# A mixture-of-experts step in split fp32: gate and up units of all four experts ahead of the down units, hidden rows turned two experts at a time

## The reference, cut to what matters

```python
gsel = jnp.argmax(glog, axis=-1)                    # one group of 4 experts for a token
gate = jnp.sum(one_hot(eidx, N_EXPERTS) * (gw * top_p)[..., None], axis=1)
hid = silu(einsum('nd,edf->nef', x, w_g)) * einsum('nd,edf->nef', x, w_u)     # d = 1024, f = 256
y = einsum('nef,efd->nd', hid * gate[..., None], w_d)
```

## Time and profile before

| what | value |
|---|---|
| median of 3 runs | 1677.16 us (1676.7 to 1677.43) |
| profiled execution, its own time | 1681.39 us |
| its span in the trace | 1679.8 us |
| TensorE busy | 98% of the span |
| VectorE, ScalarE busy | 59%, 51% of the span |

### The profile page before, as it was taken

How to read it: one execution, slowest core, us unless ns; L and a number is a source line. 1 busy time by engine, 2 the same in 40 slices (tenths; PEclk the granted TensorE clock), 3 DMA queues, 4 the chain that set the end, 5 groups by cost and what they waited for, 6 DMA issues and landing times.

```text
span 1679.8 us, 26741 instructions
## 1 busy us (share of the span) xinstructions
PE 1651.4 (98%) x9997; PEld 1337.1 (80%) x9997; DVE 996.9 (59%) x1662; ACT 862.5 (51%) x1455; POOL 642.7 (38%) x408
## 2 busy tenths in 40 slices
PE   8999999999999999999999999999999999999998
PEld 7788887777888887777778888777778888877776
DVE  3137567564451179999860384765634503999997
ACT  2443344544443347888644343554445333588884
POOL 0644454335467711000125455543345766100002
PEclk9999999999999999999999999999999999999999
DMA  9723343353556569999865233333354564799994
GB/s 353 268 89 110 107 151 128 105 181 140 191 206 244 210 217 398 391 375 379 309 228 188 101 117 121 130 120 144 138 182 162 199 242 160 267 407 376 383 368 161
DMA packets 128112, 367.23 MB, mean 219 GB/s; under 512 B 12028, under 2 KB 42364, under 8 KB 128000
## 3 DMA queue, kind: packets, MB, share of 16 engines
q1 hardware_dynamic: 93872, 319.80, 51.7%
q10 hardware_dynamic: 27504, 21.74, 4.1%
q0 software_dynamic: 6624, 24.18, 3.8%
HBM read 341.71 MB, written 23.97 MB: 218 GB/s over the span
## 4 chain that ended last, share of the span: by engine, by line
PE 84%; DVE 8%; ACT 2%; issue 2%; DMA 2%; POOL 1%; SPq 1%; POOLq 0%; DVEq 0%; ACTq 0%
PE G L1391 20%; PE G L1393 19%; PE G L1392 19%; PE S L1391 3%; PE S L1393 3%; PE S L1392 3%; DVE wlo L1930 2%; DVE pA L1930 2%; PE T L1717 2%; PE O L1467 2%; PE O L1748 2%; PE S L1703 2%; DMA x_scratch<-pA 2%; DVE prob L1930 1%; PE T L1621 1%
## 5 line engine op out<-in xcount | busy, mean ns | idle before, releaser
L856 POOL TENSOR_TENSOR wlo<-raw,whi 128x1024 fp32r<-128x1024 f32 x198 | 489.0, 2475 | 558.1 <-ACT whi L1005 557.9
L1391 PE MATMUL G<-whi,hhi 128*128 128x512 f32 (+1 forms) x1440 | 578.4, 402 | 10.3 <-DVE wlo L1930 5.5
L1393 PE MATMUL G<-whi,hlo 128*128 128x512 f32 (+1 forms) x1440 | 558.3, 388 | 0.0
L1392 PE MATMUL G<-wlo,hhi 128*128 128x512 f32 (+1 forms) x1440 | 557.8, 387 | 0.0
L1391 PEld LDWEIGHTS G<-whi,hhi 128*128 128x128 f32 x1440 | 271.0, 188 | 85.6 <-issue 16.4
L1393 PEld LDWEIGHTS G<-whi,hlo 128*128 128x128 f32 x1440 | 270.8, 188 | 57.5
L1392 PEld LDWEIGHTS G<-wlo,hhi 128*128 128x128 f32 x1440 | 271.6, 189 | 46.8
L1005 ACT ACTIVATE whi<-raw 128x1024 fp32r<-128x1024 f32 x204 | 214.8, 1055 | 98.6 <-PE G L1393 66.5
L1930 DVE TENSOR_TENSOR wlo<-raw,whi 128x1024 fp32r<-128x1024 f32 x150 | 181.7, 1225 | 13.3 <-ACT whi L1013 9.2
L1013 ACT ACTIVATE whi<-raw 128x1024 fp32r<-128x1024 f32 x144 | 152.5, 1060 | 28.6 <-PE G L1393 16.5
L1930 DVE TENSOR_TENSOR wlo<-pA,whi 128x1024 fp32r<-128x1024 f32 x72 | 88.0, 1225 | 29.3 <-ACT whi L1013 24.5
(11 more groups left out here) (405 smaller groups left out, 2292.1 us busy)
## 6 DMA issues: line engine op xcount, KB each, us to landing
raw<-in_units SPq DMA_DIRECT2D x423, 512.0 KB, 5.1
pA<-in_units SPq DMA_DIRECT2D x78, 512.0 KB, 5.9
pB<-in_units SPq DMA_DIRECT2D x72, 512.0 KB, 6.1
h_sorted<-sig POOLq DMA_DIRECT2D x12, 514.0 KB, 6.4
hs<-h_sorted POOLq DMA_DIRECT2D x10, 514.0 KB, 7.3
y_sorted<-yo POOLq DMA_DIRECT2D x10, 512.0 KB, 6.9
bias<-in_nat_bias ACTq DMA_DIRECT2D x16, 256.0 KB, 3.4
pB<-rows_scratch ACTq DMA_DIRECT2D x8, 512.0 KB, 9.1
```

Source lines behind the costliest of these rows:

```text
L856: lo_done.of(nc.gpsimd.tensor_tensor(wlo[:, k, :], raw[:, POS_OF[g] % RAW, :], whi[:, k, :].bitcast(F32), ALU.subtract))
L1391: nc.tensor.matmul(dst, st_hi, mv_hi, start=start, stop=False)
L1392: nc.tensor.matmul(dst, st_hi, mv_lo, start=False, stop=False)
L1393: return nc.tensor.matmul(dst, st_lo, mv_hi, start=False, stop=stop)
```

## The change

The order of units in a tile becomes sixteen gate and up units of the four experts, and then the eight down units. Hidden rows are turned two experts at a time: `turn_hid` issues four transposes of 128x128, after place 9 for experts 0 and 1 and after place 17 for experts 2 and 3, and the copy to ehi and the subtraction to elo take 128x512 in place of 128x256. ehi and elo hold all four experts of the tile (512 columns in place of 384 allocated). TURN_NEXT is 17 in place of 18, so the eight transposes of the next tile's rows follow the second group directly. LAST_SEL is 9 in place of 8. The units' order in memory follows the table.

```diff
-UNITS = [(_e, _u) for _e in (0, 1) for _u in range(4)] + [(0, 4), (0, 5)]
-UNITS += [(_e, _u) for _e in (2, 3) for _u in range(4)]
-UNITS += [(_e, _u) for _e in (1, 2, 3) for _u in (4, 5)]
+PAIRS = GRP // 2
+UNITS = [(_e, _u) for _e in range(GRP) for _u in range(4)]
+UNITS += [(_e, _u) for _e in range(GRP) for _u in (4, 5)]
 GATED = [UNITS.index((_e, 3)) for _e in range(GRP)]
-TURN_HID = (5, 11, 15, 19)
-TURN_NEXT = 18
+TURN_HID = (9, 17)
+TURN_NEXT = 17
...
-                            def turned_hid(e):
-                                act.wait_ge(*e_pt.in_tile(l, i, GRP, e))
-                                e_hh.of(nc.scalar.activation(ehi[:, :, e % 2 * P:(e % 2 + 1) * P], T[:, 0, 0:2 * P]
+                            def turned_hid(q):
+                                act.wait_ge(*e_pt.in_tile(l, i, PAIRS, q))
+                                e_hh.of(nc.scalar.activation(ehi[:, :, 2 * q * P:2 * (q + 1) * P],
...
-                        def turn_hid(i, e):
-                            pe.wait_ge(*e_hid.in_tile(l, i, GRP, e))
-                            pe.wait_ge(*e_hl.in_tile(l, i, GRP, e - 1))
+                        def turn_hid(i, q):
+                            pe.wait_ge(*e_hid.in_tile(l, i, GRP, 2 * q + 1))
+                            pe.wait_ge(*e_hl.in_tile(l, i, PAIRS, q - 1))
                             for f in range(2):
-                                mm = nc.tensor.transpose(T[:, 0, f * P:(f + 1) * P], hid[:, e % 2, f * P:(f + 1) * P],
-                                                         ident[:, :])
+                                for h in range(2):
+                                    mm = nc.tensor.transpose(T[:, 0, (2 * f + h) * P:(2 * f + h + 1) * P],
+                                                             hid[:, h, f * P:(f + 1) * P], ident[:, :])
...
                                 if u == 4:
-                                    pe.wait_ge(*e_hl.in_tile(l, i, GRP, e))
+                                    pe.wait_ge(*e_hl.in_tile(l, i, PAIRS, e // 2))
...
-                            def turned_hid(e):
-                                dve.wait_ge(*e_hh.in_tile(l, i, GRP, e))
-                                part = slice(e % 2 * P, (e % 2 + 1) * P)
+                            def turned_hid(q):
+                                dve.wait_ge(*e_hh.in_tile(l, i, PAIRS, q))
+                                part = slice(2 * q * P, 2 * (q + 1) * P)
```

More of the change, by code:

```diff
@@ L70 @@
 OVER = NT - GRP
-UNITS = [(_e, _u) for _e in (0, 1) for _u in range(4)] + [(0, 4), (0, 5)]
-UNITS += [(_e, _u) for _e in (2, 3) for _u in range(4)]
-UNITS += [(_e, _u) for _e in (1, 2, 3) for _u in (4, 5)]
+PAIRS = GRP // 2
+UNITS = [(_e, _u) for _e in range(GRP) for _u in range(4)]
+UNITS += [(_e, _u) for _e in range(GRP) for _u in (4, 5)]
 GATED = [UNITS.index((_e, 3)) for _e in range(GRP)]
-TURN_HID = (5, 11, 15, 19)
-TURN_NEXT = 18
+TURN_HID = (9, 17)
+TURN_NEXT = 17
 LEAD = 6
 assert LEAD <= min(GATED + list(TURN_HID)) + 3
-LAST_SEL = 8
+LAST_SEL = 9
 ROW = D + GRP
@@ L327, in program @@
         kT = sb("kT", [P, 4, TILES * P + PAST])
-        ehi = nc.alloc_sbuf_tensor_at("ehi", [P, 2, TILES * P], F32R, offset=kT_at)
-        elo = nc.alloc_sbuf_tensor_at("elo", [P, 2, TILES * P], F32R, offset=kT_at + 4 * 2 * TILES * P)
+        ehi = nc.alloc_sbuf_tensor_at("ehi", [P, 2, GRP * P], F32R, offset=kT_at)
+        elo = nc.alloc_sbuf_tensor_at("elo", [P, 2, GRP * P], F32R, offset=kT_at + 4 * 2 * GRP * P)
         hn = nc.alloc_sbuf_tensor_at("hn", [P, TILES, ROW], F32, offset=bhi0_at)
@@ L1298, in silu @@
                                 e_silu.of(nc.scalar.activation(gact[:, e % 2, :], G[:, e % 2, 0:DEXP], ACT.Silu))
-                            def turned_hid(e):
-                                act.wait_ge(*e_pt.in_tile(l, i, GRP, e))
-                                e_hh.of(nc.scalar.activation(ehi[:, :, e % 2 * P:(e % 2 + 1) * P], T[:, 0, 0:2 * P]
-                                                             .rearrange("p (f n) -> p f n", f=2), ACT.Copy))
+                            def turned_hid(q):
+                                act.wait_ge(*e_pt.in_tile(l, i, PAIRS, q))
+                                e_hh.of(nc.scalar.activation(ehi[:, :, 2 * q * P:2 * (q + 1) * P],
+                                                             T[:, 0, :].rearrange("p (f n) -> p f n", f=2), ACT.Copy))
                             for n in range(3, UT):
@@ L1791, in down @@
                             pe.wait_ge(*e_lo.in_tile(l, i, UT, n))
-                            part = slice(e % 2 * P, (e % 2 + 1) * P)
+                            part = slice(e * P, (e + 1) * P)
                             for hf in range(2):
@@ L2334, in hidden @@
                                                                 ALU.mult, ALU.mult))
-                            def turned_hid(e):
-                                dve.wait_ge(*e_hh.in_tile(l, i, GRP, e))
-                                part = slice(e % 2 * P, (e % 2 + 1) * P)
-                                e_hl.of(tt(elo[:, :, part], T[:, 0, 0:2 * P].rearrange("p (f n) -> p f n", f=2),
+                            def turned_hid(q):
+                                dve.wait_ge(*e_hh.in_tile(l, i, PAIRS, q))
+                                part = slice(2 * q * P, 2 * (q + 1) * P)
+                                e_hl.of(tt(elo[:, :, part], T[:, 0, :].rearrange("p (f n) -> p f n", f=2),
                                            ehi[:, :, part].bitcast(F32), ALU.subtract))
```

## The result

The changed kernel takes 1683.88 us (median of 8 runs) against 1677.3 us of the kernel before (8 runs): 1.0037 of its time, 95% interval 1.0027 to 1.0047, so about 6 us slower. A second measurement of both, on one chip with the experiments, gave 1.0030 (1.0020 to 1.0040). I had forecast 1679.2 us with a range to 1682.5, as no difference. The second measurement's median, 1681.48 us, lies within that range, the first one's does not.

What follows compares the result with a forecast made beforehand. TensorE, busy 98% of the span, was taken to bound the kernel. Middle tiles +1.2, last tiles -0.2 and first tiles +1.0 gave +2.0 us on 1677.16, so 1679.2 us, range 1673.5 to 1682.5.

Steps and rivals of the forecast that it cites:

- Price of transposes: TensorE, middle tile: four after place 9 cost 0.46 us, twelve after place 17 cost 1.31; fewer interruptions save 0.07.
- Waits at 6 and 14: TensorE waits for wlo at places 6 and 14, no longer covered by turns: 0.23 and 0.22 us added.
- Wait at 21: TensorE waits 0.26 us at place 21, as wide elo and two hlo stand ahead of wlo(21) on VectorE.
- Middle tile: Sum of costs and savings in a middle tile: +0.15 us each, +1.2 for eight.
- First tile, but for hs: Each layer's first tile: wide elo behind the tables delays place 13 by 0.6 us; +0.5 each, +1.0 for two.
- the waits at 6, 14 and 21 are there: Against the rival that ScalarE and VectorE queues catch up and these waits vanish: 1671.6 us, chance 12%.
- the wide elo was 0.68 long: Against the rival that the wide subtraction on VectorE costs two narrow ones, 0.84 us: 1682.1 us, chance 18%.
- four transposes cost 0.44 and not 0.24: Against the rival that a TensorE interruption is paid at its beginning, four transposes costing 0.24: 1676.6 us, chance 10%.
- The 0.3 us of VectorE time that the pairing saves in a tile: VectorE: two narrow subtractions made into one save 0.15 us, 0.3 a tile; helps only where VectorE is late.
- one or two places earlier at most: GpSimd's gates and SyncE's loads hang on the same e_hid and wlo, moved this little; no cost counted.
- the term of the last tiles: Each layer's last tile, with no hlo and so no wait at place 21: -0.1 us each, -0.2 for two.
- The waits at places 8 and 22: TensorE waits for elo at these down units, 0.25 and 0.24 us, which the change removes, 0.49 a tile.

Runs made afterwards that it cites:

- the singles: The changed kernel's unit order with hidden rows turned one expert at a time, singles17_f19 and singles18_f19: ratios 0.9990 and 0.9984 to the kernel before.
- next18_f19: Changed kernel with the next tile's rows turned after place 18 instead of 17, after 19 in first tiles: ratio 1.0009 to the kernel before.
- singles17_f19: Changed kernel, hidden rows turned one expert at a time after places 5, 9, 13, 17; next tile's rows after 17, first tiles 19: 0.9990 of before.
- tables11: first19 with the routing tables on VectorE after place 11 instead of 12: ratio 1.0007 to the kernel before.
- again: The changed kernel itself, unedited, measured a second time on one chip with the experiments: ratio 1.0030 to the kernel before.
- old_hs_twice: The kernel before, with hs of tile 1 loaded twice in a row so that it lands later: ratio 1.0118 to the kernel before.
- hs_free: Changed kernel with tile 1's hs loaded from the weights at once, not behind the scatter's landing: ratio 1.0020 to the kernel before.
- carry_memset: Changed kernel with the GpSimd 128x1 multiplication ahead of tile 1's row load replaced by a fill that reads nothing: ratio 1.0014 to before.
- first19: Changed kernel with the next tile's rows turned after place 19 instead of 17 in each layer's first tile only: ratio 1.0013 to before.
- singles18_f19: singles17_f19 with the next tile's rows turned after place 18 instead of 17: ratio 0.9984 to the kernel before.
- best11: singles18_f19 with the routing tables on VectorE after place 11 instead of 12: ratio 0.9977, 1673.89 us against 1677.7 for the kernel before.

## Why the prediction was wrong

**The steps that held.** *Price of transposes*: 0.44 and 1.32 us measured against 0.46 and 1.31, so the pairing gives hardly anything by itself. *Waits at 6 and 14*: 0.23 and 0.23 against 0.23 and 0.22, and the singles showed that the short turns cover them. *Wait at 21*: 0.22 against 0.26, gone in next18_f19. *Middle tile*: +0.16 on average against +0.15; eight of them +1.3 against +1.2. *First tile, but for hs*: +0.59 and some +0.5 against +0.5 each. None of the rivals came true: the waits at 6, 14 and 21 are there, the wide elo was 0.68 long, and four transposes cost 0.44 and not 0.24. The 0.3 us of VectorE time that the pairing saves in a tile bought nothing.

**The step that failed, first:** the sentence that GpSimd's gates and SyncE's loads hang on the same signals "one or two places earlier at most". It put the transfer of hs at nothing. It looked at what the moved turn signals and not at what it waits for: `turn` begins with a wait for hs_in. The moved TURN_NEXT and the interruptions taken out ahead of it bring TensorE to this wait 0.6 us sooner, and in a layer's first tile the transfer behind it has just landed. The price is 2.1 to 2.2 us in layer 1 (41.62 against 39.53 and 39.45 without the wait).

The trace of before had a part of it to be read: loads issued at 641.0 and 1464.8 us, 7.4 and 7.1 us to land, turns at 648.9 and 1473.9, so a room of 0.4 and 1.9 us. By these alone a turn 0.6 us sooner costs 0.2 us in layer 0 and nothing in layer 1 (an estimate). The rest needs the load to go out late, which the multiplication held for 2.31 us did. Which layer pays is luck as far as the traces show: in the changed kernel the multiplication started 22.68 us from the start of layer 0's experts and took 0.19 us, and 22.82 us from that of layer 1's and took 2.31. In singles17_f19 and tables11 it is held in layer 0 as well (2.15 and 2.25 us); their turns come later, and nothing waits.

**The second,** the term of the last tiles: -0.1 each forecast, +0.3 measured. Three of its parts were off. The waits at places 8 and 22 that I let the change remove, 0.25 and 0.24, cost only 0.12 and 0.07 in the last tile of before. Place 8 started there 0.05 us after its elo:

```profile
811.39 0.42 DVE L1930 TENSOR_TENSOR elo<-T,ehi 128x256 fp32r<-128x256 f32 x1
```

```profile
811.86 0.50 PE L1391 MATMUL S<-whi,ehi 128*128 128x512 f32 x1
```

In the middle tile it started 0.22 after the earlier trace rows, which I took to be the wait for elo. The waits of that stretch name no engine for it: three times in 108 us the first down unit's weights waited on "issue", 0.4 us at most.

```profile
PEld S L1391 <- issue: 1.3, 3, 0.4
```

Middle tiles run in a loop and the last does not; whether the loop's waits make the difference was not tried. Place 22 was late in middle tiles for the two hlo ahead of its elo, and a last tile has no hlo. I used that for place 21 and forgot it for place 22.

The third part is a wait that I had put at nothing. Place 20 is the first to need the rows of the second pair. In a middle tile twelve transposes stand ahead and give the wide elo time; in the last tile only four do, and place 20 waits 0.15 us. In the changed kernel:

```profile
830.15 0.68 DVE L1931 TENSOR_TENSOR elo<-T,ehi 128x512 fp32r<-128x512 f32 x1
```

```profile
830.89 0.50 PE L1391 MATMUL S<-whi,ehi 128*128 128x512 f32 x1
```

By the prediction's own count this elo ends 2.50 + 0.69 = 3.19 us after the moment from which it counts, and TensorE is at place 20 after 0.46 + 2.73 = 3.19, so it could have been seen. The three make some 0.45 us a tile, of which 0.4 is the miss measured: two tiles, +0.8 us.

**The sum:** 2.0 forecast; 2.2 for hs and 0.8 for the last tiles make 5.0; 5.16 measured in the experts. The two medians of the first measurement differ by 6.6 us, those of the second by 3.7; the experts' 0.31% lies within the intervals of both. The ratios agree with the experts' sums, each within its interval:

| kernel | experts against before, us | as a share of the time | ratio measured |
|---|---|---|---|
| changed | +5.2, again +5.4 | +0.31%, +0.32% | 1.0037, 1.0030 |
| old_hs_twice | +20.3 | +1.21% | 1.0118 |
| hs_free | +2.8 | +0.17% | 1.0020 |
| carry_memset | +2.9 | +0.17% | 1.0014 |
| first19 | +2.7 | +0.16% | 1.0013 |
| next18_f19 | +1.7 | +0.10% | 1.0009 |
| tables11 | +2.1 | +0.13% | 1.0007 |
| singles17_f19 | -2.8 | -0.17% | 0.9990 |
| singles18_f19 | -3.5 | -0.21% | 0.9984 |
| best11 | -3.9 | -0.23% | 0.9977 |

Theory U, an excess that is spread, fell with first19 and hs_free: their ratios of 1.0013 and 1.0020 lie under its 1.003 with their whole intervals.

## What to carry to other kernels

An interruption is worth counting only net of what it covers: two transposes of 0.24 us stood exactly where the engine would have waited 0.23 for its next operand, and taking them out gave nothing. When a step is moved forward, list what it waits for as well as what it signals, and look at the first and last round of a loop apart from the middle ones: there a transfer with a chain of its own may set the earliest time. A small operation in front of such a transfer belongs to the chain, with the longest time that it has taken beside the other engines and not with the one that a single trace shows.

## What the runs showed of the hardware

A GpSimd multiplication of 128x1 took 0.18 to 0.21 us when nothing held it. Beside fp32 subtractions of 128x1024 on VectorE (1.22 us each) it ended 0.05 or 0.06 us after one of them had ended, in all of 320 cases in twelve traces. That made up to 1.29 us behind one subtraction and 2.03 to 2.31 us where two stood back to back and it missed the gap between them; why it got through behind the first of two in the kernel before (0.24 us) is open. A fill of the same column took 0.10 us beside such a subtraction. As the operation stands ahead of a transfer, its length goes into the time at which the data lands. A TensorE wait of 7.76 us was followed by matmuls at a granted clock of 0.50, the 1.2 GHz level, in the kernel with the doubled load; after one of 2.00 us in the changed kernel the granted clock was 1.00 (1473.4 to 1478 us), the 2.4 GHz level.
